# A hybrid decoder step: the 16 by 16 diagonal blocks of the GDN systems move from TensorE squarings to forward substitution on VectorE

## The chip, the cores and the metric

One core of one Trainium2 chip runs the whole program. The metric is the device time of one execution in microseconds (us), as the median of several runs. The kernel before has a median of 1986.11 us over 3 runs (1983.29 to 1987.94).

## What is computed

Two decoder layers run over 256 prompt tokens and 8 sample tokens together. Each layer projects the normalised input once (88 tiles of 128 output channels, contraction 1024), feeds three mixers (dilated attention, GLA, gated DeltaNet = GDN), merges them, and runs a feed-forward part (layer 0 dense, layer 1 mixture of experts). Everything is float32. The change lies in GDN, whose prompt part is, for each head and chunk of tokens:

```python
dec = jnp.exp(jnp.where(incl, b[..., :, None] - b[..., None, :], -jnp.inf))
kk = jnp.einsum('bhtd,bhsd->bhts', kc, kc)
mat = eye + jnp.where(strict, bc[..., :, None] * dec * kk, 0.0)
rhs = bc[..., None] * (vc - jnp.exp(b)[..., None] * jnp.einsum('bhtd,bhdv->bhtv', kc, S))
u = lax.linalg.triangular_solve(mat, rhs, left_side=True, lower=True, unit_diagonal=True)
```

There are 4 heads. `mat` is a unit lower triangular matrix, and the kernel solves the system by its explicit inverse.

## The kernel before, in words

**Chunks.** The kernel takes the 256 prompt tokens as TT = 2 chunks of 128, so there are 2 layers x 2 chunks x 4 heads = 16 matrices of 128 by 128. A tile of four heads is 128 partitions by 512.

**Inverse.** With A the strictly lower part, `gdn_a` on VectorE (DVE) masks A and its transpose AT to the 16 by 16 diagonal blocks (Pm, PT) and starts X = I - Pm and XT = I - PT. Three steps `gdn_sq` square Pm on TensorE (PE) and add the products to X and XT, which ends in the exact inverse of each 16 by 16 block. Three levels `gdn_lv` then join blocks of 16 to 32, 64 and 128. `gdn_st` applies XT to the right side, makes the output and the state. Squarings and their products are issued by the helper `heads` (matmul at L904): one matmul per head and product, and each float32 matmul of this form leaves two records in the trace.

**Order.** Every engine runs one list, written by `schedule(l)`, and calls its own function for each step. `("proj", j)` is one of the 88 input projections, eight matmuls over 264 columns (L860, 16 records). `around(step)` puts the first half of a projection behind the step, then the step's second part (`gdn_sq2`, `gdn_lv2`...), then the other half. So the small GDN products alternate with half projections, and the half projection is what PE does while DVE or ScalarE (ACT) evacuates a product. 21 projections stand ahead of the first `gdn_dec`. Per chunk: `gdn_dec`, one projection, `gdn_a`, 3 x `gdn_sq`, 3 x `gdn_lv`, `gdn_st`, the last eight each around one projection.

**Memory.** The sync queue (SP) loads the projection weights in chunks of two projections (1 MB) into a ring of 5 slots; a load waits until PE is done with the chunk that held the slot (L710). Behind each load SP issues copies of the sample caches from input to output in memory (L748), two of about 1 MB in layer 0 and one in layer 1. GpSimd (POOL) issues the other transfers from its own queue; in the stretch around GDN these are `conv_t` (L2570 to L2572), and `gs_d` (L2588) after GDN.

**Banks.** PSUM banks 0 and 1 belong to the projections; the other six go round in the order of the jobs. ACT copies each projection out of its bank (L1578).

```python
for i in range(TT):
    s += [("gdn_dec", i)] + p() + around("gdn_a", i)
    for q in range(3):
        s += around("gdn_sq", i, q)
    for v in range(3):
        s += around("gdn_lv", i, v)
    s += around("gdn_st", i)
```

Of the kernel before, what the change touches and what calls it, by code (L numbers as in the profile page):

```python
# [10 lines left out]
P = 128  # L11
# [30 lines left out]
K_NAMES = ["ident", "ones", "blk", "upper", "neg_t", "pos_s", "m16", "m16t", "m32t", "m64t", "m128t", "hmap",  # L42
# [30 lines left out]
def schedule(l):  # L73
# [44 lines left out]
def mixer_jobs(step):  # L118
# [97 lines left out]
    ebr_ready=2, t1_ready=2, dec_ready=2, x0_ready=2, ot_ready=6, r_ready=2, qe_ready=1, dlx_ready=2, dl_ready=2,  # L216
# [9 lines left out]
def constants():  # L226
# [17 lines left out]
    put("m16", (low & (row // 16 == col // 16)) * 1.0)  # L244
    put("m16t", (low & (row // 16 == col // 16)).T * 1.0)
# [34 lines left out]
def build(nc, a, o):  # L280

    ctx = ExitStack()
    with ctx:
# [48 lines left out]
        blast, eblast, dl = cs.take(4), cs.take(4), cs.take(4)  # L332
# [25 lines left out]
        Y, R, U, kd = [v3(zc.take(512), 4) for _ in range(4)]  # L358
        zg = z[:, Z_G:Z_N, :].rearrange("p a b -> p (a b)")
# [67 lines left out]
        cache_in = [sem(f"cache_in{n}") for n in range(12)]  # L427
        stored = {n: sem(f"stored_{n}") for n in ("k0", "k1", "k2", "k3", "k4", "v", "conv", "gdn", "gdns", "gla", "glas", "toks", "copy0", "copy1",
# [194 lines left out]

        drow = nc.dram_tensor("bias_rows", [24, 512], F32, kind="Internal").ap()
# [149 lines left out]
        def _(pe):  # L774
# [149 lines left out]
            def gdn_sq(l, i, q):  # L924
                if q == 0:
                    pe.wait_ge(sems["x0_ready"], V("x0_ready", l, i))
                else:
                    wait_read(pe, l, "sq0", i, q - 1)
                    wait_read(pe, l, "sq1", i, q - 1)
                heads((l, "sq0", i, q), lambda n: PT[:, n, :], lambda n: Pm[:, n, :])  # L930
                if q < 2:
                    heads((l, "sq1", i, q), lambda n: Pm[:, n, :], lambda n: PT[:, n, :])

            def gdn_sq2(l, i, q):
                wait_read(pe, l, "sq0", i, q)
                if q:
                    wait_read(pe, l, "xx1", i, q - 1)
                heads((l, "xx0", i, q), lambda n: XT[:, n, :], lambda n: Pm[:, n, :])
                heads((l, "xx1", i, q), lambda n: Pm[:, n, :], lambda n: XT[:, n, :])

            def gdn_lv(l, i, v):
                pe.wait_ge(sems["ot_ready"], V("ot_ready", l, 3 * i + v))
                wait_read(pe, l, *(("xx0", i, 2) if v == 0 else ("lx0", i, v - 1)))
                heads((l, "y", i, v), lambda n: t1[:, n, :], lambda n: X[:, n, :])
# [23 lines left out]
            def gdn_st(l, i):  # L968
                pe.wait_ge(sems["r_ready"], V("r_ready", l, i))
                wait_read(pe, l, "lx1", i, 2)  # L970
                heads((l, "u", i), lambda q: XT[:, q, :], lambda q: R[:, q, :])

            def gdn_st2(l, i):
# [5 lines left out]
                for q in range(CH):  # L979
                    o_ = bank(l, "oc", i)[:, P * q:P * q + P]  # L980
                    last = mm(o_, U[:, q, :], QK[:, q, :], start=True, stop=(i == 0))
# [543 lines left out]
            def experts():  # L1525
# [6 lines left out]
                with pe.Else():  # L1532
# [4 lines left out]
                       gdn_sq=gdn_sq, gdn_sq2=gdn_sq2, gdn_lv=gdn_lv, gdn_lv2=gdn_lv2, gdn_st=gdn_st, gdn_st2=gdn_st2,  # L1537
# [21 lines left out]
        def _(act):  # L1559
# [107 lines left out]
            def gdn_dec(l, i):  # L1667
                if i:
                    wait_read(act, l, "ds", i - 1)
                wait_full(act, l, "brow", i)  # L1670
                act_(ebr, v3(bank(l, "brow", i), 4), ACT.Exp).then_inc(sems["ebr_ready"], 1)
                act.wait_ge(sems["t1_ready"], V("t1_ready", l, i))
                for q in range(CH):
                    n = 4 * i + q
                    act_(QK[:, q, :], t1[:, q, :], ACT.Exp, bias=nbtok[:, n:n + 1])
# [3 lines left out]
            def gdn_a(l, i):  # L1679
                wait_full(act, l, "at", i)  # L1680
                copy(AT, v3(bank(l, "at", i), 4)).then_inc(free(l, "at", i), 1)

            def gdn_sq(l, i, q):
                wait_full(act, l, "sq0", i, q)
                if q < 2:
                    wait_full(act, l, "sq1", i, q)
                copy(Pm, v3(bank(l, "sq0", i, q), 4)).then_inc(free(l, "sq0", i, q), 1)
# [127 lines left out]
            def hidden(l, i):  # L1815

                wait_full(act, l, "fg", i)
                if i >= 4:
# [9 lines left out]
                       norm_sum=norm_sum, gdn_dec=gdn_dec, gdn_a=gdn_a, gdn_sq=gdn_sq, gdn_lv=gdn_lv, gdn_st=gdn_st,  # L1828
# [110 lines left out]
        def _(dve):  # L1939
# [105 lines left out]
            def gdn_dec(l, i):  # L2045
# [7 lines left out]
                cp(blast, b_[:, :, P - 1]).then_inc(free(l, "brow", i), 1)  # L2053
# [691 lines left out]
```

## Time and profile before

| what | value |
|---|---|
| median of 3 runs | 1986.11 us (1983.29 to 1987.94) |
| the profiled execution's own time | 1977.88 us |
| its span in the trace | 1976.0 us |
| busy share PE / DVE / ACT / POOL | 96% / 26% / 19% / 6% |
| mean granted TensorE clock | 0.986 |
| mean DMA rate | 285 GB/s |

The trace is of one execution; the time around its span is 1.88 us. Times in the trace count from the span's start. GDN of layer 0 lies at about 119 to 232 us, that of layer 1 at about 935 to 1050 us. A PE record has a duration that overlaps with the next, so the pace of a stretch is read from the distance of starts.

### The profile page before, as it was taken

What the parts mean: (1) busy time and instruction counts of PE and PEld (TensorE: products, weight loads), DVE (VectorE), ACT (ScalarE), POOL (GpSimd) and SP (SyncE); (2) the same over time, 40 slices, a digit from 0 to 9 for tenths busy, and PEclk for the clock granted to TensorE, in tenths of its full rate; (3) what the DMA queues carried; (4) which work ended last, traced back from release to release, by engine and by line L of the source; (5) the groups of instructions that cost most, each with busy time, mean ns of one, the idle gap of its engine ahead of it and who ended that gap; (6) DMA issues with size and microseconds to landing.
All of it is one profiled execution on the core that took longest, in us unless ns stands there. A gap on an engine that the chain in (4) does not pass through costs nothing.

```text
span 1976.0 us, 28794 instructions
## 1 busy us (share of the span) xinstructions
PE 1898.1 (96%) x12304; PEld 1330.4 (67%) x12304; DVE 507.6 (26%) x1051; ACT 372.9 (19%) x766; POOL 121.7 (6%) x206
## 2 busy tenths in 40 slices
PE   8999999999899999999999999998879999999998
PEld 5789888787488888878998787776633343433434
DVE  3423342435331000043335324373220000000000
ACT  2132143423101000013223343310010100100101
POOL 3000000303200000000000010131000000000000
PEclk9999999999899999999999999999989999999999
DMA  9999689999979988567445677564529999779993
GB/s 304 350 364 357 250 310 336 324 330 360 392 238 386 361 281 306 201 236 267 171 157 181 223 260 259 188 235 149 198 81 358 371 376 408 276 265 387 372 408 124
DMA packets 254054, 563.10 MB, mean 285 GB/s; under 512 B 11630, under 2 KB 149074, under 8 KB 253649
## 3 DMA queue, kind: packets, MB, share of 16 engines
q1 hardware_dynamic: 235232, 500.14, 70.6%
q0 software_dynamic: 17904, 57.79, 8.7%
q10 hardware_dynamic: 784, 3.25, 0.5%
q8 instruction: 101, 1.65, 0.3%
q14 instruction: 33, 0.26, 0.0%
HBM read 547.35 MB, written 196.24 MB: 376 GB/s over the span
## 4 chain that ended last, share of the span: by engine, by line
PE 91%; DMA 3%; DVE 2%; issue 1%; SPq 1%; ACT 1%; POOL 0%; DVEq 0%; ACTq 0%; POOLq 0%
PE PS L860 29%; PE PS L1418 15%; PE PS L787 8%; PE PS L1444 7%; PE PS L904 4%; PE PS L1282 4%; PE PS L1322 4%; PE PS L780 3%; PE PS L1296 3%; PE PS L1380 2%; PE PS L897 2%; PE PS L1466 1%; PE PS L1253 1%; DMA ring<-in_w_in 1%; SPq L748 1%
## 5 line engine op out<-in xcount | busy, mean ns | idle before, releaser
L860 PE MATMUL PS<-h,ring 128*128 128x264 f32 x2816 | 660.3, 390 | 6.7 <-DMA ring<-in_w_in 6.7
L860 PEld LDWEIGHTS PS<-h,ring 128*128 128x128 f32 x2816 | 527.7, 191 | 112.2 <-issue 21.3
L1578 ACT COPY z<-PS 128x264 f32<-128x264 f32 (+3 forms) x307 | 130.7, 444 | 884.3 <-PE PS L860 555.0
L1418 PE MATMUL PS<-ring,z 128*32 128x512 f32 (+1 forms) x1440 | 212.0, 526 | 1.4 <-ACT z L1578 1.4
L1418 PE MATMUL PS<-arena,z 128*32 128x512 f32 (+1 forms) x1056 | 190.2, 535 | 0.0
L1418 PEld LDWEIGHTS PS<-ring,z 128*32 128x32 f32 x1440 | 68.0, 111 | 127.8 <-issue 112.4
L787 PE MATMUL PS<-h,ring 128*128 128x264 f32 x512 | 115.3, 386 | 1.6 <-DVE h L1971 1.6
L787 PEld LDWEIGHTS PS<-h,ring 128*128 128x128 f32 x512 | 97.3, 190 | 18.5 <-issue 2.0
L1444 PE MATMUL PS<-arena,z 128*32 128x512 f32 x432 | 104.0, 593 | 0.0
L1418 PEld LDWEIGHTS PS<-arena,z 128*32 128x32 f32 x1056 | 54.9, 110 | 54.0 <-issue 53.9
L1282 PE MATMUL PS<-z,ring 128*128 128x264 f32 x384 | 87.3, 388 | 0.0
L1418 PE MATMUL PS<-z 128*32 128x512 f32 x576 | 84.7, 593 | 0.0
L1444 PE MATMUL PS<-ring,z 128*32 128x512 f32 x480 | 83.5, 592 | 0.0
L1282 PEld LDWEIGHTS PS<-z,ring 128*128 128x128 f32 x384 | 72.4, 190 | 13.7 <-issue 1.7
L904 PEld LDWEIGHTS PS<-arena 128*128 128x128 f32 x528 | 64.9, 192 | 5.6 <-DVE arena L2069 3.3
L904 PE MATMUL PS<-arena 128*128 128x128 f32 x528 | 65.8, 276 | 1.6 <-DVE arena L2069 1.6
L1575 ACT ACTIVATE z<-PS 128x264 f32<-128x264 f32 x102 | 38.8, 390 | 150.5 <-PE PS L787 144.6
L1322 PE MATMUL PS<-z,ring 128*128 128x264 f32 x288 | 64.4, 386 | 0.0
L1575 ACT ACTIVATE z<-x 128x264 f32<-128x264 f32 x32 | 13.5, 423 | 262.8 <-DVE x L2399 174.7
L1444 PE MATMUL PS<-z 128*32 128x512 f32 x432 | 62.9, 593 | 0.0
L1296 PE MATMUL PS<-z,ring 128*128 128x264 f32 x256 | 59.5, 387 | 2.0 <-DVE z L2392 2.0
L1322 PEld LDWEIGHTS PS<-z,ring 128*128 128x128 f32 x288 | 54.8, 190 | 9.3
(315 smaller groups left out, 1788.6 us busy)
## 6 DMA issues: line engine op xcount, KB each, us to landing
out_win_s<-in_cache_win_kv SPq DMA_DIRECT2D x128, 1023.5 KB, 10.6
ring<-in_w_in SPq DMA_DIRECT2D x88, 1024.0 KB, 5.6
out_win_s<-in_cache_win_kv SPq DMA_DIRECT2D x32, 1022.0 KB, 10.6
ring<-in_moe_w_gate SPq DMA_DIRECT2D x28, 1024.0 KB, 9.6
arena<-in_moe_w_up SPq DMA_DIRECT2D x22, 1024.0 KB, 11.9
ring<-in_moe_w_up SPq DMA_DIRECT2D x22, 1024.0 KB, 8.5
ring<-in_moe_w_down SPq DMA_DIRECT2D x20, 1024.0 KB, 11.1
arena<-in_moe_w_down SPq DMA_DIRECT2D x18, 1024.0 KB, 10.5
```

Source lines behind the costliest of these rows:

```text
L780: return tr(out, in_, ident[0:rows, 0:rows])
L787: last = mm(bank(*job)[:, 0:T], w(k), h[:, k, :], start=(k == 0), stop=(k == KT - 1))
L860: last = mm(bank(l, "p", j)[:, 0:T], w[:, k, P * (j % 2):P * (j % 2) + P], h[:, k, :], start=(k == 0), stop=(k == KT - 1))
L897: mm(bank(l, "n4", n, t)[:, 0:T], K(N4[n][2]), sq4(n)[:, t, :], start=True, stop=True).then_inc(full(l, "n4", n, t), 1)
L904: last = mm(bank(*job)[:, P * q:P * q + P], left(q), right(q), start=True, stop=True)
L1282: last = mm(bank(l, "mb", b, d)[:, 0:T], v3(chunk(ch[k // 2]), 2)[:, k % 2, P * d:P * d + P], src[b][:, k, :], start=(k == 0), stop=(k == 3))
L1296: last = mm(bank(l, "wo", d)[:, 0:T], w[:, k, P * (d % 2):P * (d % 2) + P], z[:, k, :], start=(k == 0), stop=(k == KT - 1))
L1322: last = mm(bank(0, "fd", d)[:, 0:T], v3(chunk(n), 2)[:, w_, P * d:P * d + P], fa[:, k, :], start=(k == 0), stop=(k == FF // P - 1))
L1418: last = mm(m_bank("c", "gu", g, b, w, r)[BLK * j:BLK * j + BLK, 0:n], hs[:, k, P * r + BLK * j:P * r + BLK * j + BLK], v3(slot_ap(set_slo ...
L1444: last = mm(m_bank("c", "dn", g, n)[BLK * j:BLK * j + BLK, :], fc[:, k, P * r + BLK * j:P * r + BLK * j + BLK], v3(slot_ap(set_slot(SET_EG ...
L1575: return nc.scalar.activation(out, in_, func, **kw)
L1578: return nc.scalar.copy(out, in_)
```

## The change

Per chunk, DVE multiplies A by a mask of -1 on the strictly lower part of each diagonal block (`low16`) into U and sums that over the block columns, so that each row keeps its 16 values (`cut16`, 128 x 4 x 16). POOL stores them to memory, one DMA per chunk. When both have landed, POOL loads them back with one block per partition (64 partitions x 256). DVE solves all 64 blocks at once, row by row: 15 rows, each a multiply and a sum, each waiting for the one before. It adds a transposed copy, POOL stores both to memory and loads them back in the old layout, two DMAs per chunk. `fill` spreads them into X and XT with a mask (`bd16`). The three `gdn_sq` steps go. Both chunks' `gdn_dec` and `gdn_a` now come first, then `gdn_inv` and six whole projections, then the levels and states of both chunks. QK, AT, X and XT exist once per chunk.

```diff
     for i in range(TT):
         s += [("gdn_dec", i)] + p() + around("gdn_a", i)
-        for q in range(3):
-            s += around("gdn_sq", i, q)
+    s += [("gdn_inv",)] + p(6)
+    for i in range(TT):
         for v in range(3):
             s += around("gdn_lv", i, v)
         s += around("gdn_st", i)
```

TensorE:

```diff
-            def gdn_sq(l, i, q):
-                if q == 0:
-                    pe.wait_ge(sems["x0_ready"], V("x0_ready", l, i))
...
-                heads((l, "sq0", i, q), lambda n: PT[:, n, :], lambda n: Pm[:, n, :])
-                if q < 2:
-                    heads((l, "sq1", i, q), lambda n: Pm[:, n, :], lambda n: PT[:, n, :])
-
-            def gdn_sq2(l, i, q):
...
-                heads((l, "xx0", i, q), lambda n: XT[:, n, :], lambda n: Pm[:, n, :])
-                heads((l, "xx1", i, q), lambda n: Pm[:, n, :], lambda n: XT[:, n, :])
...
             def gdn_lv(l, i, v):
                 pe.wait_ge(sems["ot_ready"], V("ot_ready", l, 3 * i + v))
-                wait_read(pe, l, *(("xx0", i, 2) if v == 0 else ("lx0", i, v - 1)))
+                if v:
+                    wait_read(pe, l, "lx0", i, v - 1)
```

ScalarE (the copies of `gdn_sq` go too):

```diff
             def gdn_dec(l, i):
-                if i:
-                    wait_read(act, l, "ds", i - 1)
...
+                if i:
+                    act.wait_ge(sems["blocks"], V("blocks", l, i - 1))
```

VectorE:

```diff
             def gdn_a(l, i):
...
-                link(tt(Pm, A, bc(K("m16"), 1, [P, 4, P]), MUL))
-                tt(X, bc(ident, 1, [P, 4, P]), Pm, SUB)
-                wait_read(dve, l, "at", i)
-                link(tt(PT, AT, bc(K("m16t"), 1, [P, 4, P]), MUL))
-                tt(XT, bc(ident, 1, [P, 4, P]), PT, SUB).then_inc(sems["x0_ready"], 1)
...
+                link(tt(U, A, bc(K("low16"), 1, [P, 4, P]), MUL))
+                nc.vector.tensor_reduce(cut16[:, i], U.rearrange("p h (b c) -> p h c b", c=16), axis=AX.X,
+                                        op=ADD).then_inc(sems["blocks"], 1)
+
+            def gdn_inv(l):
+
+                link(nc.vector.memset(blk_x[:, 0, :], 0.0))
+                link(nc.vector.memset(blk_x[:, 0, 0:256:17], 1.0))
+                x_ = blk_x[:, 0, :].rearrange("p (j c) -> p c j", c=16)
+                dve.wait_ge(blocks_moved, 128 * l + 48)
+                for r in range(1, 16):
+                    t_ = blk_t[:, 0:r * r].rearrange("p (c j) -> p c j", c=r)
+                    link(tt(t_, x_[:, 0:r, 0:r], bc(blk_a[:, 16 * r:16 * r + r], 1, [64, r, r]), MUL))
+                    link(nc.vector.tensor_reduce(blk_x[:, 0, 16 * r:16 * r + r], t_, axis=AX.X, op=ADD))
+                cp(blk_x[:, 1, :].rearrange("p (c j) -> p c j", c=16), x_).then_inc(sems["blocks"], 1)
...
+                        fill(l, i)
+                level(l, 0, 0)
+
+            def fill(l, i):
+
+                dve.wait_ge(blocks_moved, 128 * l + 96 + 32 * i)
+                for w, x in enumerate((X[i], XT[i])):
+                    tt(x.rearrange("p h (b c) -> p h b c", c=16), inv16[:, w, i].unsqueeze(2).to_broadcast([P, CH, 8, 16]),
+                              v3(K("bd16"), 8).unsqueeze(1).to_broadcast([P, CH, 8, 16]), MUL)
...
             def gdn_lv(l, i, v):
                 wait_full(dve, l, "y", i, v)
                 if v < 2:
-                    level(l, v + 1)
+                    level(l, i, v + 1)
+                elif i + 1 < TT:
+                    wait_read(dve, l, "at", i + 1)
+                    level(l, i + 1, 0)
...
+                if v == 0 and i == 0:
+                    dve.wait_ge(stored["conv"], 48 * (l + 1))
+                    wait_read(dve, l, "at", 1)
+                    fill(l, 1)
```

GpSimd:

```diff
+            def gdn_a(l, i):
+                pool.wait_ge(sems["blocks"], V("blocks", l, i))
+                pool.dma_start(cuts[i].rearrange("h p c -> p h c"), cut16[:, i]).then_inc(blocks_moved, 16)
+
+            def gdn_inv(l):
+                pool.wait_ge(blocks_moved, 128 * l + 32)
+                pool.dma_start(blk_a, cuts.rearrange("i h (b r) c -> (i h b) (r c)", r=16)).then_inc(blocks_moved, 16)
+                pool.wait_ge(sems["blocks"], V("blocks", l, 2))
+                pool.dma_start(invs.rearrange("w i h (b r) c -> (i h b) w (r c)", r=16), blk_x).then_inc(blocks_moved, 16)
+                for i in range(TT):
+                    pool.wait_ge(blocks_moved, 128 * l + 64 + 32 * i)
+                    for w in range(2):
+                        pool.dma_start(inv16[:, w, i], invs[w, i].rearrange("h p c -> p h c")).then_inc(blocks_moved, 16)
```

## Rows read from the trace of the kernel before

**Rows 1.** The page: the chain that ended last, share of the span by engine

```profile
PE 91%; DMA 3%; DVE 2%; issue 1%; SPq 1%; ACT 1%; POOL 0%; DVEq 0%; ACTq 0%; POOLq 0%
```

**Rows 2.** Waits of SP in total: engine, line, released by, us, times, longest

```profile
SPq L710 <- PE PS L860: 711.5, 79, 20.1
```

**Rows 3.** Timeline, PE, layer 0, first chunk: start, us, line, records

```profile
119.74 1.05 PE L904 MATMUL PS<-con,small 128*128 128x128 f32 x8
...
128.20 1.95 PE L860 MATMUL PS<-h,ring 128*128 128x264 f32 x8
130.55 2.05 PE L904 MATMUL PS<-arena 128*128 128x128 f32 x16 [0.40 <-DVE arena L2069]
...
134.22 1.95 PE L904 MATMUL PS<-arena 128*128 128x128 f32 x16
136.00 1.95 PE L860 MATMUL PS<-h,ring 128*128 128x264 f32 x8
```

**Rows 4.** The line L904 by itself: who released it

```profile
  DVE arena L2069: 4.9, 8
```

**Rows 5.** Timeline, DVE, layer 0, first chunk

```profile
127.13 0.68 DVE L2065 TENSOR_TENSOR arena<-arena,con 128x512 f32<-128x512 f32 x1
127.85 0.69 DVE L2066 TENSOR_TENSOR arena<-con,arena 128x512 f32<-128x512 f32 x1
```

**Rows 6.** Timeline, DVE, short operations each waiting for the last

```profile
1057.70 0.20 DVE L2166 TENSOR_TENSOR arena<-arena 128x32 f32<-128x32 f32 x1
1057.93 0.19 DVE L2167 TENSOR_TENSOR arena<-arena 128x32 f32<-128x32 f32 x1
```

**Rows 7.** DVE groups by shape: a strided product

```profile
L2008 DVE TENSOR_TENSOR arena<-arena,small 128x384 f32<-128x384 f32 x2 | 1.6, 824 | 0.1
```

**Rows 8.** DMA issues by window (85:100, 230:240, 905:915, 1050:1055, 1118:1123): KB, us to landing

```profile
out_conv_p<-arena POOLq DMA_DIRECT2D x1, 18.0 KB, 8.1
...
out_gdn_p<-arena POOLq DMA_DIRECT2D x1, 256.0 KB, 5.3
...
out_conv_s<-arena POOLq DMA_DIRECT2D x1, 48.0 KB, 4.5
...
out_gdn_p<-arena POOLq DMA_DIRECT2D x1, 256.0 KB, 3.9
...
out_gla_p<-arena POOLq DMA_DIRECT2D x1, 128.0 KB, 2.2
```

**Rows 9.** Timeline, POOL: one DMA issue of 512 pieces

```profile
1050.64 0.79 POOL L2588 DMA_DIRECT2D out_gdn_p<-arena  x1 [139.41 <-DVE arena L2133]
```

**Rows 10.** Busy times by stretch; the last three columns: granted clock, DMA share, GB/s

```profile
140.00:161.40 21.40, 21.40 (x140) 19.64 (x138) 7.43 (x14) 3.81 (x8) 0.00 (x0) 1.00 1.03 354
230.00:240.00 10.00, 10.00 (x114) 8.70 (x113) 2.11 (x11) 1.43 (x4) 0.79 (x1) 1.00 0.80 303
1013.00:1034.00 21.00, 21.00 (x138) 19.33 (x137) 7.72 (x15) 3.68 (x8) 0.00 (x0) 1.00 0.38 128
```

**Rows 11.** Timeline, PE: a projection behind an idle stretch, and one in steady work

```profile
76.51 5.34 PE L860 MATMUL PS<-h,ring 128*128 128x264 f32 x16 [3.33 <-DMA ring<-in_w_in]
116.18 3.73 PE L860 MATMUL PS<-h,ring 128*128 128x264 f32 x16
530.52 1.91 PE L1253 MATMUL PS<-arena 128*32 128x512 f32 x2 [6.04 <-DMA arena<-in_cache_win_kv]
```

**Rows 12.** A stretch of 1 us, columns as in rows 10

```profile
535.00:536.00 1.00, 1.00 (x3) 0.14 (x2) 0.00 (x0) 0.00 (x0) 0.00 (x0) 0.50 1.02 369
```

**Rows 13.** Timeline, SP, layer 0: a weight load and the copies behind it

```profile
139.48 0.58 SPq L710 DMA_DIRECT2D ring<-in_w_in  x1
140.11 8.21 SPq L748 DMA_DIRECT2D out_win_s<-in_cache_win_kv  x2
```

**Rows 14.** DMA issues of the windows 139.4:140 and 360:373: KB, us to landing

```profile
ring<-in_w_in SPq DMA_DIRECT2D x1, 1024.0 KB, 14.9
...
small<-in_b_lr_bias POOLq DMA_DIRECT2D x1, 1.0 KB, 11.4
```

More of the change, by code:

```diff
@@ L243, in constants @@
     low = col < row
-    put("m16", (low & (row // 16 == col // 16)) * 1.0)
-    put("m16t", (low & (row // 16 == col // 16)).T * 1.0)
+    put("low16", (low & (row // 16 == col // 16)) * -1.0)
+    put("bd16", (row // 16 == col // 16) * 1.0)
     for b in (32, 64, 128):
@@ L331, in build @@
         btok, nbtok, ebtok, nebtok = cs.take(8), cs.take(8), cs.take(8), cs.take(8)
-        blast, eblast, dl = cs.take(4), cs.take(4), cs.take(4)
+        blast, dl = cs.take(8), cs.take(4)
         rowmax, rowsum, rowinv = cs.take(16), cs.take(16), cs.take(16)
@@ L345, in build @@
         c = v3(cc.take(12 * T), 12)
-        ebr, t1, A, QK, AT, Pm, PT, X, XT, qe, S = [v3(cc.take(512), 4) for _ in range(11)]
+        ebr, t1, A, QK0, AT0, QK1, AT1, X0, XT0, qe, S = [v3(cc.take(512), 4) for _ in range(11)]
         ucat = cc.take(12 * 32)
         catS = ucat.rearrange("p (j b k) -> p j b k", j=12, b=8)
+        XT1 = v3(arena[:, cc.at:cc.at + 512], 4)
         convt = cc.take(CCH, 24)
+        QK, AT, X, XT = (QK0, QK1), (AT0, AT1), (X0, A), (XT0, XT1)
+        cut16 = qe.rearrange("p a b -> p (a b)")[:, 0:P].rearrange("p (i h c) -> p i h c", i=TT, h=CH)
+        inv16 = qe.rearrange("p a b -> p (a b)")[:, P:3 * P].rearrange("p (w i h c) -> p w i h c", w=2, i=TT, h=CH)
         s_bc = cc.take(64).rearrange("p (n b h) -> p n b h", n=2, b=8)
@@ L980, in gdn_st2 @@
                     o_ = bank(l, "oc", i)[:, P * q:P * q + P]
-                    last = mm(o_, U[:, q, :], QK[:, q, :], start=True, stop=(i == 0))
+                    last = mm(o_, U[:, q, :], QK[i][:, q, :], start=True, stop=(i == 0))
                     if i:
@@ L1680, in gdn_a @@
                 wait_full(act, l, "at", i)
[L1681 to L1687, printed above, removed]
+                copy(AT[i], v3(bank(l, "at", i), 4)).then_inc(free(l, "at", i), 1)
             def gdn_lv(l, i, v):
@@ L1827, in _ @@
             run = dict(tables=tables, small_turn=small_turn, proj=proj, conv_a=conv_a, cz=cz, gate_c=gate_c, norm_sq=norm_sq,
-                       norm_sum=norm_sum, gdn_dec=gdn_dec, gdn_a=gdn_a, gdn_sq=gdn_sq, gdn_lv=gdn_lv, gdn_st=gdn_st,
+                       norm_sum=norm_sum, gdn_dec=gdn_dec, gdn_a=gdn_a, gdn_lv=gdn_lv, gdn_st=gdn_st,
                        gs_a=gs_a, gs_b=gs_b, gla_g=gla_g, gla_b=gla_b, gla_e=gla_e, gla_vb=gla_vb, gla_k=gla_k,
@@ L2694, in _ @@
             load_states(0)
-            run = dict(conv_t=conv_t, gs_d=gs_d, gx_q=gx_q, kv_tok=kv_tok, att_sc=att_sc, as_t=as_t, bar=bar, wo=wo)
+            run = dict(conv_t=conv_t, gdn_a=gdn_a, gdn_inv=gdn_inv, gs_d=gs_d, gx_q=gx_q, kv_tok=kv_tok, att_sc=att_sc, as_t=as_t, bar=bar, wo=wo)
             for l in range(DEPTH):
```

73 lines of the change are left out of this document (30 added, 43 removed).

## The prediction

> **What bounds the kernel now.** I read the page first: the chain that ended last. PE carries 91% of the chain, so the time is the sum of what PE has to issue [rows 1]. Then the waits of the sync queue: SP stood 711.5 us in all waiting for projections to give back ring slots, so over the span the weights wait for PE, not PE for the weights [rows 2]. Work taken off PE should therefore shorten the end, unless PE is made to wait in its place. Then the timeline of PE through GDN: small products and half projections follow each other at 1.78 us per 16 records, without a gap but one [rows 3]. GDN on PE is bound by issue, and its DVE and ACT steps are hidden under the half projections.
>
> **What is removed.** Per chunk and layer, the squarings are five groups of four matmuls (two, two, one) and their products six groups: 44 matmuls, 88 records. Over 2 chunks and 2 layers that is 352 records. Sixteen records of this form take 1.78 us (134.22 to 136.00) [rows 3], so 352 take 39.3 us. All of it lies on PE's path. The one gap goes too: PE waits for L2069 before the first squaring. The half projection at 128.20 is over at 129.98 and the squaring starts at 130.55 [rows 3]: 0.57 us, at each of the four places (8 waits in the row, a weight load and a matmul each) [rows 4], 2.3 us. Removed in all: 41.6 us. The copies and additions that leave DVE and ACT were hidden and give nothing.
>
> **What is moved.** Six whole projections (25 to 30 of each layer) now stand in one piece: 6 x 3.57 = 21.4 us at the same pace. They need only the copies of ACT, which waits for nothing of the new chain. The levels and the state keep their order and their half projections. The second chunk's `gdn_dec` comes before the first chunk's levels; its ACT part waits for the first chunk's cut, done by then. The wait of `fill(1)` on DVE stands behind the first level's additions. What it waits for is sent one hop after the first chunk's blocks, while PE does about 7.6 us of the first level; the next thing PE needs from DVE is already out or comes 2 us later. I count it as nothing, at most 1.4 us (two products) in layer 0. POOL's queue holds nothing behind these waits until `gs_d`, after GDN.
>
> **What is added, and where PE waits for it.** The end of the new chain is `level(l, 0, 0)` on DVE: until then PE stands at `gdn_lv(0, 0)`. Take layer 0 in the clock of the trace. The first `gdn_dec` starts on PE at 119.74 [rows 3]. A chunk's front is 0.89 + 3.57 + 1.78 + 1.78 + 0.45 + 1.78 = 10.25 us of PE at that pace (4, 16 and 8 records), so the second starts at 129.99, and PE is through the six projections at 129.99 + 10.25 + 21.4 = 161.6. In the first chunk the mask of L2065 starts at 127.13 and the next waiting operation at 127.85 [rows 5]. With U in its place and a sum of 512 elements behind it, the cut is ready at 128.57, 8.8 us after the start. For the second chunk that is 138.8. The cover is 161.6 - 138.8 = 22.8 us.
>
> The chain behind the cut has four hops through memory in a row: cuts out, blocks in, inverses out, inverses in. Beside them:
> - the solve on DVE. Operations of 32 elements that wait for each other start 0.23 us apart [rows 6], those of 512 elements 0.72 us [rows 5]: 0.20 us each and 1.02 ns per element. Thirty operations with 2 x 1240 elements (the squares of 1 to 15, twice) and the copy of 256 make 6.0 + 2.5 + 0.5 = 9.0 us. The multiply reads every 16th element. A product with a stride of 12 took 824 ns for 384 elements [rows 7], 1.6 ns each; if the multiplies, the copy and the cut pay that, the chain is 1.2 us longer per layer, the upper bound. The lower is nothing, as no shorter small operation is in the rows.
> - two `fill` products and the level: 3 x 0.7 = 2.1 us [rows 5].
> - the second of the two loads of the first chunk is issued behind the first: 0.8 us, from a store of as many pieces [rows 9].
>
> That is 11.9 us, so PE's stall is 4 hops + 11.9 - 22.8 = 4 hops - 10.9 us.
>
> **A hop.** No transfer of 64-byte pieces written to memory is in the trace, so I bound it by POOL's small transfers. In layer 0 one took 8.1 us in the window 85:100 and one 5.3 us at 234; in layer 1 4.5 beside a load and 3.9 us; the shortest was 2.2 us on idle DMA engines [rows 8]. The state of the DMA engines decides. Where the chain will lie in layer 0, their share is 1.03, because SP sends two copies behind each load and is blocked for 8.2 us doing so; around the 5.3 us it is 0.80 [rows 10, 13]. In layer 1 the share is 0.38 at 128 GB/s. Six projections in one piece pull a load and a copy, 2 MB, every 7.1 us, 287 GB/s, so it comes near 0.8 for these 21 us. I take 8.1 us in layer 0 and 4.5 us in layer 1, and 5.3 and 3.9 as lower ends, 11.4 as upper end in layer 0: a 1 KB load in a crowded stretch [rows 14].
>
> Stalls: layer 0 4 x 8.1 - 10.9 = 21.5 us, layer 1 4 x 4.5 - 10.9 = 7.1 us. The Trainium skill, "DMA: Bandwidth & Descriptors", section "Anatomy of one DMA — SWDGE (gpsimd) path", gives a transfer issued by GpSimd about 2.0 us plus its bytes at 436 GB/s, some 2.1 us here. By that there would be no stall; the rows of 3.9 to 8.1 us speak against it, the row of 2.2 us for it.
>
> **The clock.** After 3.33 us idle a projection took 5.34 instead of 3.73 us [rows 11], at the lower of the two levels, 1.2 GHz: 1.6 us. After 6.04 us idle PE restarted at 530.52 and the granted clock was still 0.50 in 535:536 [rows 11, 12]: over five us at half pace, about 3 us lost. I add 3.0 us in layer 0 and 1.6 us in layer 1; between nothing and 3 us each.
>
> **Sum.** -41.6 + 21.5 + 7.1 + 3.0 + 1.6 = -8.4 us. The profiled execution (1977.9 us) would be 1969.5; it lies 8.2 us under the median shown, so against the median, 1986.1, I predict **1977.7 us**. The gain is spent unevenly: layer 0 gives back 24.5 of 20.8 saved, layer 1 8.7 of 20.8.
>
> **Rivals.**
> - **Short hops.** With 5.3 and 3.9 us the stalls are 10.3 and 4.7, the clock 1.6 each: 18.2 back, -23.4, 1962.7 us. For it: the 5.3 us fell in a stretch that was busy for four fifths [rows 10]. Against: in the chain's stretch SP is blocked and the engines are never free.
> - **The chain is wholly hidden.** It needs hops under 2.7 us in both layers; with the 2.2 us of the row [rows 8] nothing comes back: -41.6, 1944.5 us. The page cited gives the same time by its 2.0 us. Only one row in a quiet stretch bears it out.
> - **Slower: layer 0's hops are starved by the copies.** Each load and store of a hop shares 16 busy DMA engines with copies queued deep. The point of decision: with layer 1 as forecast, the total passes 41.6 when layer 0's four hops pass 40.8 us, 10.2 each. At 11.4 [rows 14] the stall is 34.7, back 34.7 + 3.0 + 8.7 = 46.4, +4.8 us, 1990.9; with the strided rate in both layers +7.2, 1993 us. For it: 11.4 us is in the trace, and 64-byte pieces may be slower than what I take them from. Against: the 11.4 us had POOL's own stores ahead in its queue, and these hops do not.
> - **The ring binds in layer 0.** SP gets a load out every 8.8 us there [rows 13], the six projections use one up in 7.1 us. But the last of them needs the load issued at 139.48, which lands after 14.9 us at 154.4 [rows 13, 14], and PE comes to it at 129.99 + 10.25 + 17.9 = 158.1. If it came late, the wait would only take the place of stall. Price nothing, so no chance of its own.
>
> **Chances.** Forecast case (both layers stall, -20 to +4 us) 0.55, of it 0.10 within 4 us of before; short hops 0.15; hidden 0.05; slower rival 0.25, of it 0.05 within 4 us. A difference of about 0.2% (4 us) is what a measurement of this kernel can tell. That gives faster 0.65, same 0.15, slower 0.20. The range goes from short hops (1962) to the upper bounds (1991), leaving out the hidden case and the far end of the slower one. The forecast case alone is 1966 to 1990.
>
> **What would show it.** On PE: no products of Pm, 96 records of whole projections in a row, then an idle stretch before the first product of the first level, near 20 us in layer 0 and 7 us in layer 1, released by `level` on DVE, with the granted clock at 0.5 behind it. DVE: two idle stretches in `gdn_inv`, each two hops long, around 9 us of small operations. Landings of POOL's transfers near 8 and 4.5 us. I am wrong if the landings in layer 0 are near those of layer 1 (faster than forecast), if they are beyond 10 us, if the solve takes much more than 10 us, or if another idle stretch of PE appears, as at the levels of the second chunk.

## The result and the profile after

The changed kernel has a median of 1967.72 us (4 runs, 1963.64 to 1970.9) against 1986.08 us for the kernel before (4 runs): ratio 0.9905, 95% interval 0.9889 to 0.9921, 18.4 us less by the medians. Forecast were 8.4 us less. The sign and the range (1962 to 1991) held; the gain is more than double the forecast. Repeated on another occasion with 6 runs against 23, the ratio is 0.9925, interval 0.9905 to 0.9946, 10.7 to 18.9 us less. The traces below say how much of it the change can explain.

PE's busy line and the chain on the page of the changed kernel, which answer to [rows 1] and the table of before:

```profile
PE 1865.7 (95%) x11952; PEld 1296.5 (66%) x11952; DVE 502.6 (26%) x1085; ACT 366.0 (19%) x754; POOL 133.2 (7%) x222
...
PE 88%; DMA 6%; DVE 3%; issue 2%; ACT 1%; DVEq 0%; POOL 0%; ACTq 0%; POOLq 0%
```

PE issues 352 records fewer (11952 against 12304). The share of DMA on the chain that ended last rises from 3 to 6%. The eight hops of the new way through memory (four per layer; a hop is one transfer that the next step waits for) are 43 us of that, 2.2% of the span; the rest is a weight load at 44 us, long before GDN, over which this chain runs in this trace. In a second trace of the same kernel (e2) the share is 5%. The effect of the hops on PE is one line of the waits of PE (us in total, times, longest):

```profile
PE PS L910 <- DVE arena L2081: 23.6, 2, 17.1
```

The timeline of PE shows both places, layer 0 first. L866 is the projection, L910 the helper `heads`, L2081 the new `level`:

```profile
122.04 1.05 PE L910 MATMUL PS<-con,small 128*128 128x128 f32 x8
...
140.74 23.31 PE L866 MATMUL PS<-h,ring 128*128 128x264 f32 x104
181.10 2.08 PE L910 MATMUL PS<-arena 128*128 128x128 f32 x8 [17.06 <-DVE arena L2081]
182.97 1.06 PE L786 MATMUL PS<-con,arena 128*128 128x128 f32 x4
183.82 2.29 PE L866 MATMUL PS<-h,ring 128*128 128x264 f32 x8
185.95 1.05 PE L910 MATMUL PS<-z,arena 128*128 128x128 f32 x8
...
954.23 23.31 PE L866 MATMUL PS<-h,ring 128*128 128x264 f32 x104
984.09 2.07 PE L910 MATMUL PS<-arena 128*128 128x128 f32 x8 [6.56 <-DVE arena L2081]
985.95 1.06 PE L786 MATMUL PS<-con,arena 128*128 128x128 f32 x4
986.81 3.55 PE L866 MATMUL PS<-h,ring 128*128 128x264 f32 x8
990.20 1.05 PE L910 MATMUL PS<-z,arena 128*128 128x128 f32 x8
```

Behind each stall PE is slow for a while: 8 records take 1.87 us (181.10 to 182.97) instead of 0.89, and the half projection of layer 1 3.39 us instead of 1.78. The granted clock is 0.50 from 181 to 184 us and from 984 to 990 us, the lower of the two levels (1.2 GHz). The chain itself is read from POOL's timeline in layer 0, where a row starts when the transfer before it has landed or DVE is done:

```profile
141.66 0.78 POOL L2588 DMA_DIRECT2D block_cuts<-arena  x1 [9.41 <-DVE arena L2051]
149.56 0.57 POOL L2592 DMA_DIRECT2D z<-block_cuts  x1 [7.13 <-DMA block_cuts<-arena]
164.81 0.62 POOL L2594 DMA_DIRECT2D block_inverses<-z  x1 [14.68 <-DVE z L2064]
171.55 1.52 POOL L2598 DMA_DIRECT2D arena<-block_inverses  x2 [6.11 <-DMA block_inverses<-z]
```

and from DVE's: the first row of the solve, the copy that ends it, `fill` and `level`:

```profile
155.34 0.15 DVE L2062 TENSOR_TENSOR z<-z 64x1 f32<-64x1 f32 x1 [13.35 <-DMA z<-block_cuts]
...
164.14 0.37 DVE L2064 COPY z<-z 64x256 f32<-64x256 f32 x1
179.15 1.29 DVE L2076 TENSOR_TENSOR arena<-arena,con 128x512 f32<-128x512 f32 x2 [14.63 <-DMA arena<-block_inverses]
180.36 0.68 DVE L2081 TENSOR_TENSOR arena<-arena,con 128x512 f32<-128x512 f32 x1
```

Cuts out took 141.66 to 149.56, 7.9 us; blocks in 5.8 (to 155.34); the solve 9.2 (to 164.51); inverses out 6.7; the two loads in 7.6. In layer 1:

```profile
955.14 0.78 POOL L2588 DMA_DIRECT2D block_cuts<-arena  x1 [9.40 <-DVE arena L2051]
958.64 0.56 POOL L2592 DMA_DIRECT2D z<-block_cuts  x1 [2.72 <-DMA block_cuts<-arena]
970.25 0.62 POOL L2594 DMA_DIRECT2D block_inverses<-z  x1 [11.05 <-DVE z L2064]
975.43 1.52 POOL L2598 DMA_DIRECT2D arena<-block_inverses  x2 [4.57 <-DMA block_inverses<-z]
```

The hops are 3.5, 2.1 (DVE starts at 960.78), 5.2 and 6.7 us (DVE goes on at 982.14; 5.9 less the second issue). They go with how busy the DMA engines are while they run. The same four stretches, with the columns of [rows 10] (the last three: granted clock, DMA share, GB/s):

```profile
955.14:958.64 3.50, 3.50 (x17) 3.01 (x16) 0.27 (x2) 0.38 (x1) 0.78 (x1) 1.00 0.60 248
958.64:960.78 2.14, 2.14 (x11) 1.81 (x11) 0.00 (x0) 0.38 (x1) 0.56 (x1) 1.00 0.11 31
970.25:975.43 5.18, 5.18 (x25) 4.43 (x24) 0.00 (x0) 0.76 (x2) 0.62 (x1) 1.00 0.86 313
975.43:982.14 6.71, 2.10 (x10) 1.46 (x8) 0.00 (x1) 0.38 (x1) 1.52 (x2) 0.83 0.87 316
```

In layer 0 the share is 0.96 to 1.09 during all four.

For all kernels below, I measure a GDN stretch from the start of the first `gdn_dec` product to the first product of `gs_a`, the step behind GDN. Both stand once per layer in PE's timeline; in layer 0 of before they are at 119.74 and 234.40, after the change at 122.04 and 234.66.

| kernel | layer 0, us | layer 1, us |
|---|---|---|
| before | 114.66 | 114.65 |
| changed | 112.62 | 103.38 |

GDN gains 2.0 and 11.3 us, 13.3 in all. By the spans (1976.0 and 1964.8) the whole kernel gains 11.2.

### The profile page after: what moved, and what is told of

Read it like the earlier page. It is cut to its first block, busy times and chain, and to the rows that moved or that the text cites. A ratio compares the mean times of both kernels' runs of the same rounds, so it can differ in the third digit from the quotient of the medians.

```text
span 1964.8 us, 28061 instructions
## 1 busy us (share of the span) xinstructions
PE 1865.7 (95%) x11952; PEld 1296.5 (66%) x11952; DVE 502.6 (26%) x1085; ACT 366.0 (19%) x754; POOL 133.2 (7%) x222
## 4 chain that ended last, share of the span: by engine, by line
PE 88%; DMA 6%; DVE 3%; issue 2%; ACT 1%; DVEq 0%; POOL 0%; ACTq 0%; POOLq 0%
PE PS L866 27%; PE PS L1409 15%; PE PS L793 8%; PE PS L1435 7%; PE PS L1273 4%; PE PS L1313 4%; PE PS L786 3%; PE PS L1287 3%; DMA ring<-in_w_in 3%; PE PS L910 2%; PE PS L1371 2%; PE PS L903 2%; PE PS L1457 1%; PE PS L1244 1%; PE PS L1210 1%
## 5 line engine op out<-in xcount | busy, mean ns | idle before, releaser
L866 PE MATMUL PS<-h,ring 128*128 128x264 f32 x2816 | 662.0, 392 | 6.1 <-DMA ring<-in_w_in 6.1
L866 PEld LDWEIGHTS PS<-h,ring 128*128 128x128 f32 x2816 | 532.8, 192 | 115.5 <-issue 21.3
L1409 PEld LDWEIGHTS PS<-ring,z 128*32 128x32 f32 x1440 | 67.8, 111 | 127.9 <-issue 112.4
L793 PEld LDWEIGHTS PS<-h,ring 128*128 128x128 f32 x512 | 98.4, 192 | 19.1 <-issue 2.0
L1273 PEld LDWEIGHTS PS<-z,ring 128*128 128x128 f32 x384 | 72.3, 190 | 13.8 <-issue 1.7
L1313 PEld LDWEIGHTS PS<-z,ring 128*128 128x128 f32 x288 | 54.7, 190 | 9.4
L1435 PEld LDWEIGHTS PS<-ring,z 128*32 128x32 f32 x480 | 22.9, 110 | 56.6 <-issue 56.6
L1287 PEld LDWEIGHTS PS<-z,ring 128*128 128x128 f32 x256 | 48.5, 190 | 11.0 <-DVE z L2392 2.8
## 6 DMA issues: line engine op xcount, KB each, us to landing
out_win_s<-in_cache_win_kv SPq DMA_DIRECT2D x32, 1022.0 KB, 10.7
ring<-in_moe_w_down SPq DMA_DIRECT2D x20, 1024.0 KB, 11.4
arena<-in_moe_w_down SPq DMA_DIRECT2D x18, 1024.0 KB, 10.7
```

The lines of the kernel that those rows point to most:

```text
L793: last = mm(bank(*job)[:, 0:T], w(k), h[:, k, :], start=(k == 0), stop=(k == KT - 1))
L866: last = mm(bank(l, "p", j)[:, 0:T], w[:, k, P * (j % 2):P * (j % 2) + P], h[:, k, :], start=(k == 0), stop=(k == KT - 1))
L1273: last = mm(bank(l, "mb", b, d)[:, 0:T], v3(chunk(ch[k // 2]), 2)[:, k % 2, P * d:P * d + P], src[b][:, k, :], start=(k == 0), stop=(k == 3))
L1287: last = mm(bank(l, "wo", d)[:, 0:T], w[:, k, P * (d % 2):P * (d % 2) + P], z[:, k, :], start=(k == 0), stop=(k == KT - 1))
L1313: last = mm(bank(0, "fd", d)[:, 0:T], v3(chunk(n), 2)[:, w_, P * d:P * d + P], fa[:, k, :], start=(k == 0), stop=(k == FF // P - 1))
L1409: last = mm(m_bank("c", "gu", g, b, w, r)[BLK * j:BLK * j + BLK, 0:n], hs[:, k, P * r + BLK * j:P * r + BLK * j + BLK], v3(slot_ap(set_slo ...
```

## The experiments

Each row of stretches comes from that run's own profile. Where a run is compared with the changed kernel, its time is the 1965.78 us of e2, beside the 1983.5 us of before in the same runs (e1 to e4). e5 to e8 stand beside 1982.5 us of before and e9 to e12 beside 1984.7, so across these groups the ratios say more than the medians.

### e1 and e2: both kernels again, unchanged

> The kernel before, unchanged. The profiled execution of before lay 8 us under the median of its runs, so the gain of the change is 11.2 us by the two profiles and 18.4 us by the medians. If that profile was merely a lucky execution, this one has a span of 1980 us or more, ratio 1.000 within 0.002, and the extra time should sit in layer 0 before GDN or in the attention stages, where PE waits for weights or cache tiles. If profiled executions of before are shorter as a rule, its span is again 1976 us and the other runs 1985 us.

> The changed kernel, unchanged. By the traces the change is worth 13.3 us within the two GDN stretches. If that is all, the ratio is 0.9933 (1972.8 us against 1986.1). If it gives more, as the first timing said, the ratio is 0.9905 (1967.7 us), and something outside GDN gains some 5 us. The stalls should repeat: 17 us in layer 0, 6.6 us in layer 1.

Measured: before 1982.81 us in 10 runs (ratio to itself 1.0002, interval 0.9986 to 1.0018), span of the profile 1981.1. Changed 1965.78 us, ratio 0.9925. GDN stretches: before 114.65 and 114.65, changed 113.39 and 103.81, a gain of 12.1 us; the stalls are 17.8 and 6.9 us. The first profile of before (1977.88 us) was a quick execution: the runs of one kernel scatter over some 10 us (1976.57 to 1987.66). Between these two profiles 19.1 us lie, 12.1 in GDN and 7.0 elsewhere, where both kernels do the same work; between the first two profiles elsewhere was 2.1 us the other way. Part of the scatter can be seen. The 5.1 us by which the span of e1 exceeds that of the quick profile lie in sum neither before layer 0's GDN nor in the attention stages, where I had expected them, but nearly all at `gather`, a step of the mixture of experts in layer 1. Its first product starts 0.8 us later in e1 (1446.65 against 1445.81 us), and the end of the span is 5.1 us later. The code is the same and the DMA engines are idle, but the granted clock is not the same; the quick profile, then e1:

```profile
1456.00:1466.00 10.00, 8.68 (x26) 4.21 (x24) 0.00 (x0) 1.91 (x4) 0.00 (x0) 1.00 0.00 0
1456.00:1466.00 10.00, 9.34 (x21) 4.27 (x19) 0.00 (x0) 1.43 (x3) 0.00 (x0) 0.78 0.00 0
```

From that first product to the end the changed kernel and e2 both took 526.9 us, the quick profile 525.7, e1 529.9, and the variants of the changed kernel below 526.8 to 537.9, with the same code there. A smaller step is seen at one spot of the attention stage, in the quick profile of before and in e1, the same code with the same idle time of 1.57 us:

```profile
465.90 1.13 PE L1219 MATMUL PS<-arena,con 8*128 8x512 f32 x6 [1.57 <-issue]
466.97 3.83 PE L860 MATMUL PS<-h,ring 128*128 128x264 f32 x16
```

```profile
465.52 1.13 PE L1219 MATMUL PS<-arena,con 8*128 8x512 f32 x6 [1.57 <-issue]
466.58 5.51 PE L860 MATMUL PS<-h,ring 128*128 128x264 f32 x16
```

In e1 the projection behind it takes 1.7 us more, at a granted clock of 0.79 over these 2 us (the columns of [rows 10]) against 1.00 in the other:

```profile
466.00:468.00 2.00, 2.00 (x11) 1.15 (x6) 1.74 (x3) 1.99 (x2) 2.00 (x4) 0.79 0.95 301
```

So single executions differ by steps of 1.7 to 5 us that the code does not set. The figures for the change rest on the GDN stretches, whose work is fixed and which in the kernel before took 114.65 or 114.66 us in every trace.

### e3: no round trip

```diff
             def gdn_a(l, i):
...
+                if i == 0:
+                    tt(X[0], bc(ident, 1, [P, 4, P]), U, ADD)
...
-                dve.wait_ge(blocks_moved, 128 * l + 48)
-                for r in range(1, 16):
...
-                dve.wait_ge(blocks_moved, 128 * l + 96 + 32 * i)
+                if i:
+                    tt(X[i], bc(ident, 1, [P, 4, P]), U, ADD)
+                link(tt(XT[i], AT[i], bc(K("bd16"), 1, [P, 4, P]), MUL))
+                tt(XT[i], bc(ident, 1, [P, 4, P]), XT[i], ADD)
```

The mask `bd16` is changed too, to -1 on the transposed strictly lower part of each block, and POOL's transfers are gone.

> The round trip and the solve are left out; the block inverses are taken to first order (I - P), so the outputs are not the reference's. Order of work and PE's instructions are those of the changed kernel. If PE's issue is the bound and the stalls are the only price, the stalls of 17.2 and 6.6 us and their clock losses (1.7 and 3.0 us) go: 28.5 us faster than the changed kernel, 41.6 us faster than before (1944 us). Rival: in layer 0 the weights cannot keep up with the shorter PE list while SP sends copies; then PE waits for the ring in the six projections or behind them and layer 0 gives 5 us or more less, 1950 us or above.

Measured: 1941.15 us, ratio 0.9798 (0.9772 to 0.9824), 42.4 us less than before by the medians. Both GDN stretches are 93.67 us, 21.0 less than before each, 42.0 in all; no wait of PE at L910 is left. What is removed from PE arrives at the end whole, and the ring does not bind in layer 0: the rival falls. 93.67 us is the floor of a stretch, and the changed kernel stands 19.0 us above it in layer 0 and 9.7 in layer 1.

### e4: one hop more

The waits behind the load that is made twice count one transfer more.

```diff
-                pool.wait_ge(blocks_moved, 128 * l + 32)
-                pool.dma_start(blk_a, cuts.rearrange("i h (b r) c -> (i h b) (r c)", r=16)).then_inc(blocks_moved, 16)
+                for n in range(2):
+                    pool.wait_ge(blocks_moved, 144 * l + 32 + 16 * n)
+                    pool.dma_start(blk_a, cuts.rearrange("i h (b r) c -> (i h b) (r c)", r=16)).then_inc(blocks_moved, 16)
```

> The load of the blocks is made twice, one behind the other: one more hop in the chain of each layer. If the stall is the serial chain less the cover, it grows by one hop: 5.8 us in layer 0 and 3 to 4.5 us in layer 1, some 10 us slower than the changed kernel (1977 us). Rival: PE's stall in layer 0 is set by something else that comes out late there (a weight load or the copies in front of it), and layer 0 does not move; then 4 us slower.

Measured: 1978.0 us, ratio 0.9975 (0.996 to 0.999), 12.2 us more than e2 where some 10 were expected. The stalls are 29.3 and 10.3 us, 11.5 and 3.4 more than in e2. The chain is serial in both layers. Layer 0 grew by more than the added hop, and POOL's timeline of layer 0 has the reason:

```profile
147.54 0.57 POOL L2593 DMA_DIRECT2D z<-block_cuts  x1 [8.10 <-DMA block_cuts<-arena]
153.23 0.53 POOL L2593 DMA_DIRECT2D z<-block_cuts  x1 [5.12 <-DMA z<-block_cuts]
...
174.98 1.52 POOL L2599 DMA_DIRECT2D arena<-block_inverses  x2 [6.36 <-DMA block_inverses<-z]
188.70 1.49 POOL L2599 DMA_DIRECT2D arena<-block_inverses  x2 [12.20 <-DMA arena<-block_inverses]
```

The added hop is 5.7 us, but the loads back, now issued at 174.98, needed 13.7 us to the next issue; in the changed kernel the next issue came 7.9 us behind, at 179.41. The profiled execution was the slowest of the ten of e4 (1982.59 us), so this pair may be a rare one. The slow rival's 11.4 us for a hop was in reach all the same.

### e5: no copies around layer 0's chain

```diff
-                per = 1 if n >= CH_MIX or l else 2
-                if l or n >= COPY_FROM:
+                per = 1 if n >= CH_MIX + 8 or l else 2
+                if (l or n >= COPY_FROM) and not (l == 0 and 12 <= n <= 19):
```

> In layer 0, SP sends no cache copies behind eight weight loads around GDN (chunks 12 to 19); they follow in the first eight chunks of the feed-forward part and at the end of the list. If the copies' backlog is what makes layer 0's hops long, they fall from 6 to 8 us to layer 1's 2.3 to 5 us, PE's stall in layer 0 falls from 17 us to 7 us or less and the kernel is 8 to 12 us faster than the changed one (about 1956 us), unless the postponed copies cost elsewhere. Rival: a hop's length is its own latency; the stall in layer 0 stays over 14 us.

Measured: 1965.99 us, ratio 0.9915, as the changed kernel; the 8 to 12 us did not come. But the trace splits it cleanly. The stretch 140:164 (last columns DMA share, GB/s) of the changed kernel, then of e5, then e5's hops and PE:

```profile
140.00:164.00 24.00, 24.00 (x111) 20.19 (x109) 9.33 (x34) 2.85 (x7) 1.34 (x2) 1.00 1.04 356
```

```profile
140.00:164.00 24.00, 24.00 (x111) 20.21 (x109) 11.48 (x38) 2.86 (x7) 4.87 (x7) 1.00 0.50 152
```

```profile
141.69 0.78 POOL L2588 DMA_DIRECT2D block_cuts<-arena  x1 [9.41 <-DVE arena L2051]
144.14 0.57 POOL L2592 DMA_DIRECT2D z<-block_cuts  x1 [1.67 <-DMA block_cuts<-arena]
155.80 0.62 POOL L2594 DMA_DIRECT2D block_inverses<-z  x1 [11.09 <-DVE z L2064]
159.11 1.52 POOL L2598 DMA_DIRECT2D arena<-block_inverses  x2 [2.69 <-DMA block_inverses<-z]
162.62 1.49 POOL L2598 DMA_DIRECT2D arena<-block_inverses  x2 [1.99 <-DMA arena<-block_inverses]
```

```profile
164.31 1.16 PE L910 MATMUL PS<-arena 128*128 128x128 f32 x8 [0.25 <-DVE arena L2081]
```

With the share halved, the hops fall to 2.5, 2.2 (DVE starts at 146.32), 3.3 and 2.5 us (DVE goes on at 162.36, less the second issue of 0.8), PE waits 0.25 us instead of 17.06, and the GDN stretch is 94.18 us, half a microsecond above the floor. So the copies' traffic set the length of the hops in layer 0. The 18.4 us gained there were given back where the copies went: from the first feed-forward product to the first product of layer 1's GDN 336.75 us instead of 326 to 328, with PE waiting for the weights:

```profile
629.88 5.39 PE L793 MATMUL PS<-h,arena 128*128 128x264 f32 x16 [2.93 <-DMA arena<-in_ffn_w_up]
649.54 5.52 PE L793 MATMUL PS<-h,ring 128*128 128x264 f32 x16 [3.60 <-DMA ring<-in_ffn_w_up]
```

and the rest in the cache loads of both attention stages (25.1 and 20.4 us around `as_v` instead of 22.0 to 23.2 and 16.8).

### e6: four projections more as cover

```diff
-    s += [("gdn_inv",)] + p(6)
+    s += [("gdn_inv",)] + p(10)
...
-        s += p() + [("norm_sq", n)] + p() + [("norm_sum", n)]
-    s += p()
-    s += p(64 - 21 - 18 - 16 - 8) + [("kv_tok",), ("att_sc", 0)]
+        s += p() + [("norm_sq", n)] + p(n < 8) + [("norm_sum", n)]
+    s += [("kv_tok",), ("att_sc", 0)]
```

> Ten whole projections in place of six stand behind the gdn_inv step; four that stood around the last attention norms are gone from there. If the stall is the chain less the cover, 14.3 us more of cover take away the stall of layer 1 (6.7 us and 3.0 us of slow clock) and leave 3 us in layer 0: 20 us faster than the changed kernel, less what the norms now show that those projections covered, at most 1 to 2 us for each of the four places and layer. So 1950 to 1958 us. Rival: the longer piece in layer 0 runs the ring dry (a load every 8.8 us against 7.1 us of use) and PE waits for weights in it, 5 us or more.

Measured: 1964.97 us, ratio 0.9901 (0.9871 to 0.9932), against an expected 1950 to 1958 us: no gain over e2 that is clear of the noise. The stall of layer 1 is gone and that of layer 0 is 4.8 us. Without the 14.3 us of added projections the GDN stretches are 101.2 and 93.6 us: 12.2 and 10.2 us won against e2. The stretch from `gs_a` to `kv_tok` lost four projections but shrank by 6.4 us only (122.3 against 128.7), 7.9 us given back per layer. The norms now show what those projections covered:

```profile
342.42 2.05 PE L902 MATMUL PS<-z,con 128*128 128x264 f32 x8 [1.80 <-ACT z L1565]
349.82 2.05 PE L902 MATMUL PS<-z,con 128*128 128x264 f32 x8 [1.79 <-ACT z L1565]
356.26 6.02 PE L785 MATMUL PS<-con,z 128*128 128x128 f32 x27 [4.39 <-DVE z L2025]
```

Three waits, 8.0 us. By the stretches 6.6 us should remain; the medians do not show them, in runs that spread from 1957.5 to 1972.4, and the interval of e2's ratio (0.9925) overlaps this one. I had priced the uncovered norms at 1 to 2 us each and missed the last one, whose 4.39 us are the norm and the square in a row. The ring did not run dry.

### e7: from SBUF to SBUF

```diff
-                pool.dma_start(cuts[i].rearrange("h p c -> p h c"), cut16[:, i]).then_inc(blocks_moved, 16)
+                for q in range(CH):
+                    at = 32 * i + 8 * q
+                    pool.dma_start(blk_a[at:at + 8, :], cut16[:, i, q, :]).then_inc(blocks_moved, 16)
...
-                pool.dma_start(invs.rearrange("w i h (b r) c -> (i h b) w (r c)", r=16), blk_x).then_inc(blocks_moved, 16)
...
+                            pool.dma_start(inv16[:, w, i, q, :], blk_x[at:at + 8, w, :]).then_inc(blocks_moved, 16)
```

> The blocks go from SBUF to SBUF, with eight transfers in and eight per chunk out, and no memory between: two hops in the chain in place of four, but four to eight issues in a row (0.5 us each). If hops are what costs, the chain of layer 0 falls from 27 us of hops to 2 x 6 to 8 plus 2 + 4 us of issues, 18 to 22 us: 5 to 9 us off the stall in layer 0, and 2 to 5 us in layer 1. About 1957 us. Rival: many small transfers in one queue cost as much as they save: same as the changed kernel.

Measured: 1953.49 us, ratio 0.9848 (0.9821 to 0.9875), 30.1 us less than before by the ratio. The GDN stretches are 103.52 and 94.63 us, and PE's waits:

```profile
172.50 2.08 PE L910 MATMUL PS<-arena 128*128 128x128 f32 x8 [7.97 <-DVE arena L2081]
968.80 1.16 PE L910 MATMUL PS<-arena 128*128 128x128 f32 x8 [0.70 <-DVE arena L2081]
```

Nine and six microseconds off the stalls. In layer 0 the way from the second chunk's first issue (142.14) to the solve (151.32) takes 9.2 us instead of 13.7, and from the inverses' first issue (160.77) to `fill` (170.55) 9.8 us instead of 14.3, the issues of 2.35 and 4.72 us included. Two hops are gone and the row of issues costs less than they did, so the rival falls.

### e8: e6 and e7 together

> Both of the above together. No stall in either layer if both theories hold: all of the 41.6 us less 0 to 8 us of uncovered norms, 1942 to 1950 us. Rival: as for the single edits.

Measured: 1959.46 us, ratio 0.9892 (0.9875 to 0.9908), slower than e7 alone and not the 1942 to 1950 us expected. No stall is left at L910 in either layer (stretches 93.6 and 93.6 without the added projections), but the 7.9 us of bare norms come twice, 15.8 us, for 11 us of stall. Cover has to come from where it is not used already.

### e9 and e10: the copies moved to layer 1, and the control

```diff
-                per = 1 if n >= CH_MIX or l else 2
-                if l or n >= COPY_FROM:
+                per = 1 + (20 <= n < 32) if l else (1 if n >= CH_MIX else 2)
+                if l or (n >= COPY_FROM and not 13 <= n <= 18):
```

> The changed kernel, with no cache copies behind six weight loads around layer 0's GDN (chunks 13 to 18); the twelve copies go behind chunks 20 to 31 of layer 1, where the DMA engines are idle a third of the time, not into the feed-forward part. In the run that put them there, layer 0's GDN stretch fell to 94.2 us (93.7 without the round trip) but the feed-forward stretch grew by 10.7 us. If that growth was the price of the place alone, GDN of layer 0 stays near 94 to 98 us, the feed-forward stretch is 326 us again, and the kernel is 14 to 18 us faster than the changed one: 1948 to 1952 us. Rival: twice the copies cost in layer 1 what they save in layer 0; then 1960 us or more.

> The kernel before with the same moved copies, as the control. It has no chain through memory, so if the copies act on the hops alone its time is that of before within 0.3% (1982 us). If it gains 5 us or more, the copies slow something else and the gain of the quiet stretch is not due to the hops.

Measured: e9 1958.71 us, ratio 0.9887 (0.9866 to 0.9907), by the ratios 7.5 us faster than the changed kernel and not the 14 to 18 expected. The feed-forward stretch is 326.07 us again, so the growth in e5 was the price of its place. GDN of layer 0 is 105.63 us, not the 94 to 98 expected: the stall is 10.1 us. The window of six chunks is too short for the chain at both ends. SP issues its last copies before it at 114.92 to 120.63, and the DMA share is still 1.07 from 130 to 140 us: the cuts, issued at 140.90, took 5.1 us. The next copies go out at 160.17, just before the inverses at 160.63, which took 6.8 us at a share of 0.98; between, from 150 to 160 us, it is 0.35. Control e10: 1979.8 us, ratio 0.9977 (0.9965 to 0.999), with GDN stretches of 114.65 and 114.66 us. The moved copies do nothing to GDN without the chain. They do give the old kernel 2 to 7 us elsewhere, which I had not expected. By the profiles of e1 and e10 it is 1.6 us up to the first `gdn_dec`, 2.2 us between layer 0's `gs_a` and layer 1's GDN, and 1.9 us from there to `gather`. The first of these lies ahead of the moved copies and cannot be theirs; what causes the others was not tried. So of e9's gain only the GDN part is due to the hops.

### e11 and e12: direct transfers and moved copies

e11 is e7 with the edit of e9. e12 also keeps layer 1's chunks 13 to 18 free of copies:

```diff
+                per = 1 + (20 <= n < 38) if l else (1 if n >= CH_MIX else 2)
+                if (l or n >= COPY_FROM) and not 13 <= n <= 18:
```

> SBUF to SBUF transfers and the moved copies together. Direct transfers alone left a stall of 8 us in layer 0 and 1 us over the floor in layer 1. With hops of 2 to 3 us in layer 0 both stalls go: GDN stretches of 93.7 to 95 us each, and some 10 us faster than direct alone: 1941 to 1946 us, the time of the kernel without round trip. Rival: layer 1 pays for the copies, 1950 us.

> As e11, and layer 1's copies behind its chunks 13 to 18 are moved behind chunks 32 to 37 too. Layer 1's direct hops have a stall of at most 1 us left, so within 0.1% of e11. If it is slower, the copies in the later stretch of layer 1 cost something there.

Measured: 1950.42 us, ratio 0.9831 (0.9814 to 0.9848), and 1950.21 us, ratio 0.9824 (0.98 to 0.9847). GDN stretches 102.62 and 97.61 us, and 102.13 and 93.67 us. e11 misses its 1941 to 1946 us. In layer 0 the window gains 1 us over e7; 5.8 to 7.0 us of stall stay. Layer 1 has a stall of 2.0 us in e11 where e7, with the same list and copies up to there, has 0.7, so such a stretch varies by 3 us (97.61 against 94.63) from one trace to another. With the window also in layer 1 its stretch is on the floor to the hundredth, in one trace. The intervals of both overlap that of e7, so it is open whether moving the copies adds anything to the direct transfers. These are the fastest kernels that leave nothing out: some 34 us under before, against 42 us without any round trip.

## Why the prediction was wrong where it was

**What bounds the kernel, and what is removed: right.** 352 records went. Forecast 41.6 us (22 times 1.78 is 39.2 and not 39.3 us, so 41.5), measured with the chain left out 42.0 us in the GDN stretches, 42.4 us by the medians.

**What is moved: right.** The second chunk's `fill` started as soon as DVE was free (no wait of PE behind it), POOL's queue delayed nothing, ACT copied all projections in time. From the first `gdn_dec` to the end of the six projections I had 41.9 us; it was 42.0 (122.04 to 164.04, where the wait of 17.06 us begins).

**The fixed part of the chain: right.** Solve 9.2 us against 9.0. The cut was 0.3 us late: the strided sum took 1.02 instead of 0.72 us, within the bound from [rows 7]. Fill and level 1.9 against 2.1. Not in the sum was that POOL issues 0.3 us after DVE is done, twice in the chain.

**The hop in layer 0: the term that was mis-sized.** I took 8.1 us for each of four, 32.4 us; they took 7.9, 5.8, 6.7 and 6.8 (7.6 less the second issue), 27.2 us. The mechanism held: e5 shows that the copies make the hops long, 2.2 to 3.3 us without them. But one landing of an 18 KB store beside SP's backlog stood for four transfers of other kinds. Whether the kind matters is open: the blocks in took 5.8 us in the first trace and 6.9 in e2's, the inverses out 6.7 and 6.2. The stall came out at 17.1 instead of 21.5 us. The two bounds, 5.3 and 11.4, enclosed the mean of 6.8; no row said where between them it would lie. In layer 1 I had 18.0 us for four hops and the second issue's 0.8 us, 18.8 in all, and it was 17.5; the stall 6.6 against 7.1 us. There the sum was met with some luck: 4.5 us for each hop stood against 3.5, 2.1, 5.2 and 5.9. The DMA share that I expected under the six projections, near 0.8, was 0.86 and 0.87 for the last two hops, and 0.60 and 0.11 for the first two.

**The rule against the rows.** The hops were 2.2 to 3.3 us in the quiet of e5, 2.1 us for layer 1's blocks in, and 5.8 to 7.9 us under the copies, up to 13.7 us for two loads in e4. The Trainium skill's "DMA: Bandwidth & Descriptors", section "Anatomy of one DMA — SWDGE (gpsimd) path", gives 2.0 us and the bytes: near the traces in the first two cases, far from them under the copies. I was right to take the rows, as the rival of a wholly hidden chain needs DMA engines with little else to do.

**The clock: right in sum, wrong in place.** 3.0 us were meant for layer 0 and 1.6 for layer 1. Measured are 1.7 and 3.0 (each stretch less the floor and the stall gives 1.9 and 3.1). The stall of 17.1 us did not cost more than that of 6.6 us. Why not was not tried.

**The sum.** Forecast for GDN: -41.6 + 33.2 = -8.4 us. Measured there: -13.3 in the first pair of traces and -12.1 in the second. Four to five microseconds of the miss are the hops of layer 0. The other five, up to the 18.4 us of the first timing, lie outside GDN. The first timing's interval, 15.7 to 22.0 us, does not hold 13.3; the second's, 10.7 to 18.9 us, does. Less their two GDN stretches, the spans of before and e1 are 1746.7 and 1751.8 us, those of the changed kernel, e2, e3 and e4 1748.8, 1744.8, 1752.6 and 1748.9: no gain outside GDN in the traces, and the stage from `gather` on alone differs by 4 us between two traces of one kernel. So I take the five for scatter between executions. That some of it is a true side effect is not excluded.

**The rivals.** Short hops (-23.4) came nearer to the first timing (18.4) than the forecast did, which is luck: to the second (14.9 by its ratio) and to the 13.3 us in GDN the forecast was nearer, and the rival's hop of 5.3 us was not what was measured in layer 0 (6.8). The ring never bound (e3, e6).

## What to carry to other kernels

A detour through memory costs hops times the landing time under the traffic of that moment, here 2.1 us at a DMA share of 0.11 and 7.9 us at 1.09; price it by the traffic there, and carry the spread into the range. Removing work from the bound engine pays in full only if the detour is covered, and the cover must not be taken from steps that need it. A copy between SBUF partitions without the stop in memory halves the number of hops, which won more here than quieter DMA engines or more cover.

## What the runs showed that I had not expected

One code path with the same idle time before it ran at full pace in one execution and 1.7 us slower in another (e1), and `gather` took 4 us more in one than in the other, so profiles of two kernels differ outside the edit by such steps. The same two loads of layer 0, issued at 171.55 in the changed kernel, let the next issue go after 7.9 us, and in e4, issued 3.4 us later, after 13.7 us. What decides there beyond the traffic as a whole was not tried. And moving twelve copies of 1 MB from a stretch with full DMA engines to one with spare share made even the old kernel 0.23% faster (0.1 to 0.35%).
